# More expert places, a later TensorE branch, another order in the conv layers, and alpha times x by a scaled identity

## The reference, cut to what is computed

```python
ALPHA = (2 * DEPTH) ** 0.25
for i in range(DEPTH):
    mix = (_short_conv_mixer, _retention_mixer, _sgu_mixer)[i % 3](x, ...)
    x = _layer_norm(ALPHA * x + mix, ln_g[i, 0], ln_b[i, 0])
    ffn = _moe(x, router_w, router_b, moe_w_gate[i], moe_w_up[i], moe_w_down[i])
    x = _layer_norm(ALPHA * x + ffn, ln_g[i, 1], ln_b[i, 1])
    emb = p[i] @ ple_w_proj[i]
    gate = jax.nn.sigmoid(x @ ple_w_gate[i] + ple_b_gate[i])
    x = x + gate * emb
...
# _moe: hf = x (256 x 1024), combine = the two experts' weights of each token
for e in range(N_EXPERTS):
    he = jax.nn.silu(hf @ w_gate[e]) * (hf @ w_up[e])      # 1024 -> 512
    y = y + combine[:, e:e + 1] * (he @ w_down[e])         # 512 -> 1024
```

## Time and profile before

| | us |
|---|---|
| median of three runs | 1803.83 |
| lowest and highest | 1800.16, 1804.5 |
| the profiled execution | 1801.2 |
| its span, first to last instruction | 1799.4 |
| mean granted TensorE clock | 0.961 |

### The profile page before, as it was taken

How to read it: one execution, slowest core, us unless ns; L and a number is a source line. 1 busy time by engine, 2 the same in 40 slices (tenths; PEclk the granted TensorE clock), 3 DMA queues, 4 the chain that set the end, 5 groups by cost and what they waited for, 6 DMA issues and landing times.

```text
span 1799.4 us, 17844 instructions
## 1 busy us (share of the span) xinstructions
PE 1649.2 (92%) x7564; PEld 991.1 (55%) x7564; DVE 716.4 (40%) x1030; ACT 468.8 (26%) x545; POOL 16.8 (1%) x34
## 2 busy tenths in 40 slices
PE   6988999869999899997799999899986998999976
PEld 5864443258777743432588778543324877443325
DVE  3572111174757711111757656311116666111116
ACT  4531111034443311111344343211102452111111
POOL 0000000000000000000000000000000000000000
PEclk9998999979999999999899999899998998999997
DMA  7487999945443889999465446799995567899990
GB/s 278 183 315 311 421 421 421 421 166 210 166 183 129 332 355 421 422 421 421 166 257 201 148 162 273 325 422 421 421 421 217 205 231 284 356 422 421 422 388 24
DMA packets 77180, 547.99 MB, mean 305 GB/s; under 512 B 8608, under 2 KB 8608, under 8 KB 12320
## 3 DMA queue, kind: packets, MB, share of 16 engines
q1 hardware_dynamic: 73296, 530.95, 72.7%
q0 software_dynamic: 3792, 15.73, 2.4%
HBM read 545.60 MB, written 1.05 MB: 304 GB/s over the span
## 4 chain that ended last, share of the span: by engine, by line
PE 72%; DVE 12%; DMA 12%; ACT 2%; issue 2%; SPq 0%; DVEq 0%; ACTq 0%
PE psum L802 30%; PE psum L485 10%; PE psum L487 10%; PE psum L486 10%; DMA expert_high<-in_experts 6%; PE psum L794 4%; DMA expert_work<-in_experts 4%; DVE w_lo L1290 4%; PE psum L812 3%; PE psum L496 2%; ACT w_hi L1000 1%; DMA raw<-in_slots 1%; DVE work_r L1290 1%; PE psum L750 1%; DVE xT_lo L1290 1%
## 5 line engine op out<-in xcount | busy, mean ns | idle before, releaser
L1290 DVE TENSOR_TENSOR w_lo<-raw,w_hi 128x2048 fp32r<-128x2048 f32 x120 | 271.2, 2288 | 165.4 <-ACT w_hi L1000 164.5
L485 PE MATMUL psum<-w_hi,xT_hi 128*128 128x512 f32 x704 | 284.7, 404 | 17.6 <-DVE w_lo L1290 11.1
L486 PE MATMUL psum<-w_lo,xT_hi 128*128 128x512 f32 x704 | 279.8, 397 | 0.0
L487 PE MATMUL psum<-w_hi,xT_lo 128*128 128x512 f32 x704 | 279.4, 397 | 0.0
L1000 ACT ACTIVATE w_hi<-raw 128x2048 fp32r<-128x2048 f32 x120 | 225.1, 1909 | 103.4 <-PE psum L487 90.0
L802 PE MATMUL psum<-raw,xg 128*64 128x512 f32 x904 | 215.0, 599 | 7.5 <-DMA raw<-in_experts 7.4
L1000 ACT ACTIVATE work<-psum 128x512 f32<-128x512 f32 x156 | 91.0, 593 | 433.4 <-PE psum L487 207.1
L1290 DVE TENSOR_TENSOR work_r<-psum,work_r 128x512 fp32r<-128x512 f32 x84 | 56.7, 690 | 363.5 <-ACT work_r L1000 363.5
L485 PEld LDWEIGHTS psum<-w_hi,xT_hi 128*128 128x128 f32 x704 | 136.0, 193 | 51.8 <-DVE xT_lo L1290 9.4
L487 PEld LDWEIGHTS psum<-w_hi,xT_lo 128*128 128x128 f32 x704 | 135.6, 193 | 29.4
L486 PEld LDWEIGHTS psum<-w_lo,xT_hi 128*128 128x128 f32 x704 | 135.9, 193 | 28.1 <-issue 0.2
(11 more groups left out here) (143 smaller groups left out, 1364.8 us busy)
## 6 DMA issues: line engine op xcount, KB each, us to landing
raw<-in_experts SPq DMA_DIRECT2D x168, 1024.0 KB, 17.7
raw<-in_slots SPq DMA_DIRECT2D x120, 1024.0 KB, 4.9
expert_work<-in_experts SPq DMA_DIRECT2D x112, 1024.0 KB, 15.9
expert_high<-in_experts SPq DMA_DIRECT2D x104, 1024.0 KB, 17.3
ln_par<-in_ln_g POOLq DMA_DIRECT2D x8, 512.0 KB, 8.6
ln_par<-in_ln_b POOLq DMA_DIRECT2D x8, 512.0 KB, 11.4
bgate<-in_ple_b_gate POOLq DMA_DIRECT2D x4, 512.0 KB, 4.7
work<-in_c_ln_g POOLq DMA_DIRECT2D x1, 1536.0 KB, 9.1
```

The costliest lines, as they stand in the source:

```text
L485: mm(out, lhs[0], rhs[0], start=start, stop=False)
L486: mm(out, lhs[0], rhs[1], start=False, stop=False)
L487: return mm(out, lhs[1], rhs[0], start=False, stop=stop)
L1290: return tt(lo, whole, hi.bitcast(F), ALU.subtract)
```

## The change

It has five parts.

1. **Places.** 17 instead of 14: `norm` (the region of `ln_par`, which moves into the arena), `xg` 1 (the second half of the gathered tokens, where `xT_lo` lies before) and `y`. The ring has 15 places; `xg` 1 is used once, for k = 3, and `y` once, for k = 9. They are loaded out of turn: `y` when the mixer's last slot has been used, `norm` when the first norm of tile 1 is done, `xg` 1 when the logits are. GpSimd loads the second norm's parameters once the last slot in `norm` has been used (k = 74).
2. **Branch.** The put-back of the last pair now stands ahead of the branch on TensorE. The rounds for crowded experts add their results to PSUM by VectorE.
3. **Splits.** ScalarE and VectorE split the gate's first slot right after their last copy of `y`, ahead of their own branch.
4. **Order.** In the conv layers tile 0's transposes, its copies and its logits move behind the mixer's last slot and tile 1's norm. In all layers tile 1's embedding rows move behind the logits. The fourth gather goes to bank 5, and each of the first four expert slots waits for its own piece of `xg` only.
5. **Alpha.** `ident_alpha` is the identity times alpha. Behind k = 3 TensorE multiplies x by it into banks 0 to 3 (four fp32 multiplies), and the put-back adds to that. The second norm of a layer reads PSUM, with no residual step.

```diff
-        first = [*early, raw[5], raw[4], raw[3], high[3], raw[2], high[2], raw[1], high[1], *late, raw[0], high[0]]
-        last = [raw[5], raw[4], raw[3], raw[2], high[1], high[0], *work, raw[1], raw[0]]
...
+        ring = [*early, raw[5], raw[4], raw[3], high[3], raw[2], high[2], raw[1], high[1], *late, ("norm", 0),
+                raw[0], high[0]]
+        n_first = len(ring) + 2
+        turns = [k for k in range(n_first) if k not in (EARLY_K, LATE_K)]
+        at = dict(zip(turns, ring))
+        at[EARLY_K], at[LATE_K] = ("xg", 1), ("y", 0)
+        norm = ring.index(("norm", 0))
+        loads = turns[:norm] + [LATE_K] + turns[norm:norm + 1] + [EARLY_K] + turns[norm + 1:]
...
+                elif kind == "norm":
+                    sp.wait_ge(x_tile_ready, 6 * L + 2)
+                elif kind == "xg":
+                    sp.wait_ge(logitsT_in_psum, L + 1)
+                elif kind == "y":
+                    sp.wait_ge(weights_used, n)
...
-                pool.wait_ge(x_tile_ready, 6 * L + 2)
+                pool.wait_ge(experts_used, last_use(L, ("norm", 0)))
                 load_norm(L, 1)
...
-                    if i == 3:
+                    if i == 3 and L % 3:
                         transpose_tile(3 * L + 1, 0)
                     rows_slot(n, count, lhs, q, 1, i, mix_done)
+                if L % 3 == 0:
+                    transpose_tile(3 * L + 1, 0)
...
-                turned_tile(3 * L + 1, 0)
-                logits(0)
+                if L % 3:
+                    turned_tile(3 * L + 1, 0)
+                    logits(0)
                 rows_group(starts[L][1], 1, tiled(pT), 0, 0, emb_in_psum)
-                pe.wait_ge(mix_read, L + 1)
-                rows_group(starts[L][1], 1, tiled(pT), 0, 1, emb_in_psum)
                 transpose_tile(3 * L + 1, 1)
+                if L % 3 == 0:
+                    turned_tile(3 * L + 1, 0)
+                    logits(0)
                 turned_tile(3 * L + 1, 1)
                 logits(1).then_inc(logitsT_in_psum, 1)
...
+                pe.wait_ge(mix_read, L + 1)
+                rows_group(starts[L][1], 1, tiled(pT), 0, 1, emb_in_psum)
...
-                for i in range(3):
-                    gather(0, i, 5 + i)
+                for i in range(4):
+                    if i == 3:
+                        pe.wait_ge(xg_ready, 16 * L + 1)
+                    gather(0, i, (5, 6, 7, 5)[i])
                 pe.wait_ge(flag_ready, L + 1)
-                gather(0, 3, 4)
...
+                for s in range(4):
+                    pe.wait_ge(xg_ready, 16 * L + s + 1)
+                    wide(0, "gate", 4, s)
                 pe.wait_ge(emb_ready, 4 * (L + 1))
-                pe.wait_ge(xg_ready, 16 * L + 4)
-                for s in range(4):
-                    wide(0, "gate", 4, s)
+                for t in range(T):
+                    for c in range(2):
+                        mm(psum[:, 2 * t + c, :], ident_alpha[:, :], x[:, t, c * NB:(c + 1) * NB], start=True, stop=False)
...
-                def finish():
-                    pe.wait_ge(y_ready, 2 * PAIRS * (L + 1) - 1)
-                    for t in range(T):
-                        put_back(place[1], y, t, 0, False, True)
-                    pe.wait_ge(y_ready, 2 * PAIRS * (L + 1))
-                    for t in range(T):
-                        put_back(place[1], y, t, 1, False, True).then_inc(ffn_done, 1)
+                pe.wait_ge(y_ready, 2 * PAIRS * (L + 1) - 1)
+                for t in range(T):
+                    put_back(place[1], y, t, 0, False, True)
+                pe.wait_ge(y_ready, 2 * PAIRS * (L + 1))
+                for t in range(T):
+                    put_back(place[1], y, t, 1, False, True).then_inc(ffn_done, 1)
 
                 with pe.If(crowded > 0):
...
                 stop[0] = starts[L + 1][2] if L + 1 < DEPTH else n_gate + 4
+                split_behind(n_gate - 3)
...
-                save_tile(3 * L + 1, 0)
+                if L % 3:
+                    save_tile(3 * L + 1, 0)
                 wait_rows(dve, L, 1, mix_done, L + 1, end)
                 residual(1, 0)
                 layer_norm(1, 2 * L, mix_read)
+                if L % 3 == 0:
+                    save_tile(3 * L + 1, 0)
                 save_tile(3 * L + 1, 1)
...
-                residual(0, 0)
-                layer_norm(0, 2 * L + 1)
-                split_behind(starts[L][2] - 3)
+                layer_norm(0, 2 * L + 1, sums=0)
                 save_tile(3 * L + 2, 0)
                 split_behind(starts[L][2])
                 dve.wait_ge(ffn_done, T * L + 2)
-                residual(1, 0)
-                layer_norm(1, 2 * L + 1)
+                layer_norm(1, 2 * L + 1, sums=2)
```

More of the change, by code:

```diff
@@ L73, in expert_places @@
         early, late = {0: (work, []), 1: (work[2:], work[:2]), 2: (work[:3], work[3:])}[layer % 3]
-        first = [*early, raw[5], raw[4], raw[3], high[3], raw[2], high[2], raw[1], high[1], *late, raw[0], high[0]]
-        last = [raw[5], raw[4], raw[3], raw[2], high[1], high[0], *work, raw[1], raw[0]]
-        rounds = EXPERT_SLOTS // len(first)
-        assert len(set(first)) == len(first) and len(last) == EXPERT_SLOTS - rounds * len(first)
-        out.append(first * rounds + last)
+        ring = [*early, raw[5], raw[4], raw[3], high[3], raw[2], high[2], raw[1], high[1], *late, ("norm", 0),
[6 more added lines that the diff above has]
+        loads = turns[:norm] + [LATE_K] + turns[norm:norm + 1] + [EARLY_K] + turns[norm + 1:]
+        k = n_first
+        while k < EXPERT_SLOTS - 5:
+            turn = ring if k + len(ring) < EXPERT_SLOTS - 5 else [p for p in ring if p[0] != "norm"]
+            for place in turn:
+                at[k] = place
+                k += 1
+        for place in [p for p in turn if p in work + raw[:2]][:5]:
+            at[k] = place
+            k += 1
+        assert k == EXPERT_SLOTS
+        out.append(([at[i] for i in range(EXPERT_SLOTS)], loads + list(range(n_first, EXPERT_SLOTS))))
     return out
@@ L399, in _ @@
                         load_x(1)
-                for k, (p, part, i) in enumerate(STREAM):
+                for k in load_order[L]:
+                    p, part, i = STREAM[k]
                     wait_place(L, k)
```

58 lines of the change are left out of this document (38 added, 20 removed).

## The result

| | before | changed |
|---|---|---|
| median, us | 1801.99 | 1785.13 |
| lowest to highest (four runs each) | 1799.68 to 1804.5 | 1782.79 to 1786.02 |
| the profiled execution | 1801.2 | 1786.02 |
| its span | 1799.4 | 1784.2 |
| mean granted clock | 0.961 | 0.963 |

(The median of before has one run more in it than ahead of the prediction.) The ratio is 0.9904, with a 95% interval of 0.9885 to 0.9923: 16.9 us faster by the medians, where 25.6 were forecast. The predicted time of 1778 was 7 us too low. The two spans differ by 15.2. I split that between four stretches of each layer, all read from the timelines: from tile 0's first norm to the first expert multiply (route and gathers), from there to the last expert multiply (the stage), from there to tile 1's second norm (the tail), and the remainder (gate and next mixer).

The account below looks back on a forecast made before the run. DMA was taken to bound the end of each expert stage, by 7.2 us per layer, with a serial tail behind. (1.5 + 0.9 + 4.0) x 4 = 25.6 us off 1801.2, on the median's scale 1778; range 1766 to 1791.

Parts of the forecast that it names:

- Expert stage: Experts, each layer: slot k = 91 starts at 198.4 us from k = 0 instead of 199.96, -1.5.
- identity multiplies: TensorE, between k = 3 and k = 4: four fp32 multiplies take 3.44 us per layer.
- load 25: Expert loads: issued when k = 10 ends at 26.3, it lands 4.9 us later, at 31.2 from k = 0.
- norm load: Second norm's parameters, 1.05 MB after k = 74: they take 2.9 us of the full stream, between 0 and 2.9.
- Start of the experts: First expert matmul needs only the first gather copy and no longer waits for the last: -0.9 us per layer.
- Tail: After the last expert matmul: branch hidden, residual steps and a split gone; tile 1 comes 4.0 us earlier per layer.
- Conv order: Route of the two conv layers: 1.3 us won, set against a lower clock; counted 0, between -1.3 and +2.
- Embedding rows: Route, all layers: tile 1's rows (2.8 us) hide in the 3.66 us hole before `chosen`; nothing won, 0.
- B: Rival: norm load costs nothing, TensorE bounds k = 91 at 196.0, 9.6 us less, 1768; chance 0.15.
- D: Rival: the hole before the put-back is not the branch's, 6.4 us more, 1784; chance 0.07.
- C: Rival: idle time before the logits lowers TensorE's clock, costing 2 to 3 us per layer, 1788; chance 0.15.
- E: Rival: slower; k = 3's load lands late, TensorE stops at the fourth slot, +3.6 us per layer, 1818; chance 0.03.

Follow-up runs that it names:

- x3: Changed kernel without the loads of the second norm's gains and offsets (the gate's bias row serves for both): 1777.8 us, ratio 0.9868 to the kernel before.
- x4: Changed kernel with TensorE's branch ahead of the last put-back again: 1786.4 us, ratio 0.9914 to the kernel before.
- x1: Changed kernel with the four identity multiplies moved from behind k = 3 to behind k = 81, 82, 84 and 85: 1769.8 us, ratio 0.9822 to before.
- x12: Changed kernel with late identity multiplies, tile 1's embedding rows ahead of its transposes, and the new conv order in all layers: 1763.8 us, ratio 0.9798 to before.
- x9: Changed kernel with four more identity multiplies behind k = 3, into a bank nobody reads: 1797.0 us, ratio 0.9971 to the kernel before.
- x5: Changed kernel with the old order of tile 0's transposes, copies and logits in the two conv layers: 1785.3 us, ratio 0.9918 to before.
- x6: Changed kernel with tile 1's embedding rows ahead of tile 1's transposes again, in all layers: 1783.0 us, ratio 0.9907 to before.
- x11: Changed kernel with both the old conv order and tile 1's embedding rows ahead of its transposes: 1784.1 us, ratio 0.9907 to before.
- x7: Changed kernel without identity multiplies; VectorE adds alpha x in a residual step ahead of the second norm: 1780.8 us, ratio 0.9895 to before.
- x2: Changed kernel with the four identity multiplies right ahead of the first put-back (behind k = 15): 1779.0 us, ratio 0.9872 to before.
- x10: Changed kernel with late identity multiplies and without the second norm's parameter loads: 1765.8 us, ratio 0.9802 to the kernel before.

## Why the prediction was right or wrong

**What bounds the kernel: right.** TensorE's course to k = 80 is fixed to the hundredth, and DMA sets the end of the stage. Load for load the stream is 2.49, from load 25 to load 91 167.5 us in the mean, where 164.3 + 2.9 = 167.2 were forecast.

**Expert stage, -1.5 forecast, +1.2 measured: wrong, and this is the miss.** The identity multiplies cost their 3.44, and k = 10 ended at 26.4 (26.3). The step that failed is the next: "a transfer into an idle queue takes 4.9 from issue to landing: load 25 lands at 31.2". The queue wasn't idle: load 25 was issued 3.5 to 4.9 ahead of load 24's landing, took 7.15 in the mean, and landed at 33.6, 2.4 late. The remaining 0.3 are some 0.7 of gaps in the stream, which I had not counted, less 0.4 for the norm load, counted at 2.9 and measured at 2.5. 2.7 x 4 = 10.8, nearly the whole difference. Behind it stands a larger oversight: I had seen that the multiplies delay load 25 and priced them, yet took their place as given. Since TensorE waits 7 us for DMA at the end, there is a place where they cost nothing.

**Start of the experts, -0.9: right.** The first slot follows the gathers at once in all four layers.

**Tail, -4.0: right in layers 1 to 3.** 26.0 from the last expert multiply to tile 1's norm, against 29.5 to 30.2 before, -3.8 in the mean. The branch is hidden there. In layer 0 a hole of 2.1 was left, on which I had not counted and which the branch, ended 2.8 ahead of the transposes' `x`, doesn't explain: -2.2.

**Conv order, 0: right as a sum for the route** (the two conv layers changed by -0.0 and -1.5, of which -0.9 each was forecast for the start of the experts). The order is worth 1.0 with the rows ahead; with them behind the fold the clock takes it back or not, from one execution to the next. **Embedding rows, 0: half right.** In the changed kernel's first layer they stick out by 0.8 behind `chosen`, at the lower clock; the larger price is paid ahead of them. "So nothing is won" held. But ahead of the transposes the rows were more than hidden: behind them the logits ran at the upper clock.

**Rivals.** B and D are excluded by x3 and x4. C happened in part: by 1.8 or more in layer 3, by 0 to 3 in layer 0, and not beyond the spread in the other two; it is within the sum above. E did not: there is no wait at slot 3. That no more than 10.4 is missing in the spans is in part luck: the stage, the tail and the route fell short by 13.9 together, and 3.5 came back in the remainder, for which nothing had been forecast. Executions of the same code differ there by as much: over the changed kernel and x1 to x12 the first mixer takes 115.0 to 118.9 up to tile 0's norm, and the end behind layer 3's last norm 22.9 or 24.5.

## What to carry to other kernels

Where a stream of loads sets the end of a stage, work on the engine that frees the places is not cheap or dear by its length but by when it stands: right behind the start of the refill each microsecond of it came back at the end, and where the engine waits for the stream it was nearly free. To price a load, ask first what is in flight when it is issued, and look up a load in the same position, not one into an empty queue. When a filler is moved out of an engine's idle time, ask what that idle time does to its clock, and compare several executions before you put a number on it.

## What the runs showed of the hardware

- A 1 MiB load landed 4.7 to 4.9 after its issue into an empty queue (load 20 in the changed kernel and x9, all layers), and 6.0 to 7.9 after its issue where another was still in flight (loads 18 and 25 in the changed kernel, x1 and x9, all layers; the first layer of x1: load 18 issued at 3.69, landing at 10.92). In the full stream one landed every 2.49.
- In five of the twelve profiled kernels that have TensorE's branch behind the put-back (changed, x3, x5, x6, x11), the first layer's put-back is followed by 10.0 to 10.8 us of idle time that nothing seen ends, where the others have 7.8 up to the norm's `x` (9.0 in x7, with its residual step); never in layers 1 to 3. It wasn't isolated, and its cause is open.
- The route to the experts differs in length between executions of the same code, with the granted clock: layer 0's from tile 1's norm to k = 0 took 20.2 (changed, x1, x7, x9), 18.3 (x2, x3), 17.3 (x4) or 21.1 (x10), and the mean clock was 0.66 in the changed kernel, 0.81 in x2 and 0.63 in x10. These differences are as large as the effects that were sought there.
